# Crossings between the stages of a five-layer network: a weight split on GpSimd, tiles taken bank by bank, and the normalization folded into the turn

## The chip, the cores and the metric

The kernel runs on one core of a Trainium2 chip. The metric is the device time of one execution, in microseconds, as the median of the runs.

## The reference

A sequence of 256 tokens of 1024 features goes through four layers and then a fifth of another kind, all in 32-bit floats. Each layer is

```
h = h + 0.5 * rmsnorm(ffn(rmsnorm(h, g0)), g1)
h = h + rmsnorm(mixer(rmsnorm(h, g2)), g3)
h = h + 0.5 * rmsnorm(ffn(rmsnorm(h, g4)), g5)
```

with `ffn(x) = (silu(x @ w_gate) * (x @ w_up)) @ w_down` of 2816 hidden features, `rmsnorm(x, g) = x * rsqrt(mean(x*x) + eps) * g`, and as mixers a windowed attention (layers 0 and 3), a gated linear attention (GLA, layer 1) and an RWKV-7 time mix (layer 2). The fifth layer has the same three parts without the norm behind each (`h = h + 0.5 * ffn(rmsnorm(h, g))`) and a hybrid of two attentions as mixer; a last rmsnorm follows.

## The kernel before

Tokens lie on the partitions as two tiles of 128 (NT = 2). The sum h and the scratch y are held in SBUF, [128, 2, 1024]. To keep the precision of 32 bits every weight and every activation is split into a high part, rounded to the matmul's faster 32-bit type, and a low part (the rest), and each product is three matmuls. Weights stream in units through four raw buffers: SP issues the loads (`load_unit`, L292), ACT makes the high part (`split_high`, L264, the instruction at L269), DVE the low part (`split_low`, L271, at L273); two buffers hold split units. A raw buffer is free once `weights_split` counts its unit, and SP waits for that in order.

The work is a list of stages: "ffn" (23 units; each unit PE's gate and up matmuls at L337 and L338 and the down matmuls of the unit before at L350 to L352, tile 0 before tile 1, into four banks of PSUM, `out_banks`), "proj" (a matrix product in chunks of 256 columns, L481, into `gate_bank` or, for a mixer's last product, `out_banks`), attention and mixer stages, and "cross". Behind each stage `barrier` (L227) lets PE, ACT and DVE wait for one another except where `passes` (L234) says otherwise.

A crossing takes the result of the last product in `out_banks` (two banks a tile) to the input of the next. There are 16. 14 are turned, that is they end in a transpose: the first, which has no result to add; five behind a mixer's product; eight behind an ffn. The other two are the one into the RWKV mixer and the last. In a turned crossing with a gain:

- ACT squares tile 0 of the result and sums it (`root_of`, L549, square at L551, root at L552), then tile 1. DVE multiplies tile 1 by the gain (L610), then, once ACT has the root of tile 0, tile 0, so that the two are never at one bank. With a bias (behind attention) DVE adds it first (L601), ACT squares that sum in y, and DVE waits for ACT's drain before the gain product (L606).
- DVE: reciprocal and residual addition `h += y * rstd` (`residual`, L615, at L622) for tile 0, then tile 1. Without a norm the addition takes the result straight from PSUM (L624).
- ACT squares h for the next norm; DVE writes y = h * rstd (`normed`, L632, at L637).
- PE transposes each block of 128 columns of y with the identity (`cross_pe`, L676, at L681) into `out_banks`, eight for tile 0, then eight for tile 1.
- ACT writes the high part of x, scaled by the next gain, for each of eight blocks (L581); DVE the low part (L648). PE's next stage starts on block 0 when its low part is there.

At an ffn's end PE signals `branch_tile_ready` after the last matmul of tile 0 and `weights_used` after that of tile 1. ACT and DVE split the first unit of the next stage there (L383, L414), ahead of the crossing; where the crossing follows an ffn they have also split the first part of that stage's second unit (`split_early_high`, `split_early_low`). DVE starts such a crossing when all of the ffn's matmuls are done (L596). Behind a projection the barrier stands ahead of the crossing.

## Time and profile before

| | us |
|---|---|
| median of 3 runs | 3422.99 (3420.08 to 3426.07) |
| the profiled execution | 3428.41 |
| its span, first to last instruction | 3426.6 |

```profile
PE 2971.8 (87%) x17510; PEld 2595.5 (76%) x17510; DVE 1982.3 (58%) x2349; ACT 1435.1 (42%) x1781; POOL 0.9 (0%) x9
```

This line of the page gives each engine's busy time and its share of the span. PE is the matrix engine, PEld its weight loads, DVE the vector engine, ACT the scalar engine, POOL GpSimd; SP issues the weight loads. L numbers are lines of the kernel. In timelines a row names start, duration, engine, line, operation, output<-inputs with their shapes, a count, and in brackets how long the engine had been idle before and who released it. The granted clock of TensorE in that execution was 0.919 of full speed on the mean.

### The profile page before, as it was taken

What the parts mean: (1) busy time and instruction counts of PE and PEld (TensorE: products, weight loads), DVE (VectorE), ACT (ScalarE), POOL (GpSimd) and SP (SyncE); (2) the same over time, 40 slices, a digit from 0 to 9 for tenths busy, and PEclk for the clock granted to TensorE, in tenths of its full rate; (3) what the DMA queues carried; (4) which work ended last, traced back from release to release, by engine and by line L of the source; (5) the groups of instructions that cost most, each with busy time, mean ns of one, the idle gap of its engine ahead of it and who ended that gap; (6) DMA issues with size and microseconds to landing.
All of it is one profiled execution on the core that took longest, in us unless ns stands there. A gap on an engine that the chain in (4) does not pass through costs nothing.

```text
span 3426.6 us, 43921 instructions
## 1 busy us (share of the span) xinstructions
PE 2971.8 (87%) x17510; PEld 2595.5 (76%) x17510; DVE 1982.3 (58%) x2349; ACT 1435.1 (42%) x1781; POOL 0.9 (0%) x9
## 2 busy tenths in 40 slices
PE   6987898988589799666887898997799997978898
PEld 5876787878478688655885787886687886977887
DVE  4665666663756566655555566666566663645565
ACT  4444445443344444442221444445444443434443
POOL 0000000000000000000000000000000000000000
PEclk9997899998699999887997899999799998989999
DMA  7643565644056565320000565653365555642562
GB/s 224 184 129 99 159 189 175 184 129 148 1 172 190 145 201 166 110 86 1 1 1 20 154 184 162 202 164 106 117 184 177 177 166 138 180 132 83 176 192 92
DMA packets 639646, 471.49 MB, mean 138 GB/s; under 512 B 56002, under 2 KB 607298, under 8 KB 639509
## 3 DMA queue, kind: packets, MB, share of 16 engines
q1 hardware_dynamic: 609456, 451.00, 43.7%
q10 hardware_dynamic: 30052, 18.57, 2.2%
q8 instruction: 97, 1.59, 0.2%
q14 instruction: 41, 0.33, 0.0%
HBM read 466.63 MB, written 1.84 MB: 137 GB/s over the span
## 4 chain that ended last, share of the span: by engine, by line
PE 70%; DVE 14%; ACT 6%; PEld 4%; ACTq 3%; issue 2%; PEldq 1%; DVEq 1%; DMA 0%; SPq 0%
PE pair_bank L337 22%; PE pair_bank L338 11%; PE pair_bank L481 11%; PE out_banks L350 5%; PE out_banks L352 5%; PE out_banks L351 5%; PEld out_banks L481 3%; DVE low L273 2%; ACT high L269 2%; PEldq L229 1%; DVE mix L1896 1%; PE pair_bank L1737 1%; DVEq L229 1%; PE out_banks L681 1%; PE pair_bank L1750 1%
## 5 line engine op out<-in xcount | busy, mean ns | idle before, releaser
L273 DVE TENSOR_TENSOR low<-raw,high 128x3072 fp32r<-128x3072 f32 (+3 forms) x328 | 948.0, 2890 | 889.9 <-ACT high L269 889.9
L337 PE MATMUL pair_bank<-x_parts,high 128*128 128x512 f32 x3520 | 1247.9, 396 | 34.8 <-DVE low L273 29.6
L338 PE MATMUL pair_bank<-x_parts,low 128*128 128x256 f32 x3520 | 988.1, 281 | 0.0
L269 ACT ACTIVATE high<-raw 128x3072 fp32r<-128x3072 f32 (+3 forms) x328 | 784.9, 2393 | 402.3 <-PE out_banks L352 199.8
L337 PEld LDWEIGHTS pair_bank<-x_parts,high 128*128 128x128 f32 x3520 | 665.5, 189 | 194.8 <-DVE low L273 28.6
L338 PEld LDWEIGHTS pair_bank<-x_parts,low 128*128 128x128 f32 x3520 | 670.3, 190 | 9.3
L377 ACT ACTIVATE sq_scratch<-pair_bank 128x512 f32<-128x512 f32 x220 | 131.6, 598 | 580.4 <-PE pair_bank L338 580.4
L350 PE MATMUL out_banks<-high,hid_h 128*128 128x512 f32 x880 | 349.0, 397 | 13.0 <-DVE hid_l L411 13.0
L352 PE MATMUL out_banks<-high,hid_l 128*128 128x512 f32 x880 | 348.4, 396 | 0.0
L351 PE MATMUL out_banks<-low,hid_h 128*128 128x512 f32 x880 | 348.3, 396 | 0.0
L481 PE MATMUL pair_bank<-high,x_parts 128*128 128x256 f32 (+1 forms) x1248 | 245.7, 295 | 30.9 <-DVE low L273 17.0
L481 PE MATMUL pair_bank<-x_parts,high 128*128 128x256 f32 x1216 | 236.0, 296 | 40.2 <-DVEq L229 31.1
L481 PEld LDWEIGHTS pair_bank<-high,x_parts 128*128 128x128 f32 x1248 | 208.5, 203 | 34.4 <-DVE low L273 17.4
L481 PEld LDWEIGHTS pair_bank<-x_parts,high 128*128 128x128 f32 x1216 | 200.7, 203 | 44.6 <-issue 42.1
L350 PEld LDWEIGHTS out_banks<-high,hid_h 128*128 128x128 f32 x880 | 165.6, 188 | 56.7 <-DVE hid_l L411 9.3
L352 PEld LDWEIGHTS out_banks<-high,hid_l 128*128 128x128 f32 x880 | 165.7, 188 | 39.8
L351 PEld LDWEIGHTS out_banks<-low,hid_h 128*128 128x128 f32 x880 | 165.7, 188 | 29.9
L481 PE MATMUL pair_bank<-low,x_parts 128*128 128x256 f32 (+1 forms) x624 | 182.2, 292 | 0.0
L481 PE MATMUL pair_bank<-x_parts,low 128*128 128x256 f32 x608 | 177.8, 292 | 0.0
L379 ACT ACTIVATE silu<-sq_scratch 128x256 f32<-128x256 f32 x220 | 91.9, 418 | 183.9 <-DVE sq_scratch L402 183.9
L402 DVE TENSOR_TENSOR sq_scratch<-sq_scratch,pair_bank 128x512 f32<-128x512 f32 x220 | 151.2, 687 | 27.1 <-ACT sq_scratch L377 21.3
L405 DVE TENSOR_TENSOR hidden<-silu,sq_scratch 128x256 f32<-128x256 f32 x220 | 93.5, 425 | 106.5 <-ACT silu L379 106.5
(348 smaller groups left out, 3108.1 us busy)
## 6 DMA issues: line engine op xcount, KB each, us to landing
raw<-in_ffn_w_in_dram SPq DMA_DIRECT2D x352, 512.0 KB
raw<-in_ffn_w_out_dram SPq DMA_DIRECT2D x176, 512.0 KB
raw<-in_ffn_w_dram SPq DMA_DIRECT2D x132, 512.0 KB
raw<-in_w_in_dram SPq DMA_DIRECT2D x32, 1024.0 KB
raw<-in_gla_w_in_dram SPq DMA_DIRECT2D x12, 1024.0 KB
raw<-in_rwkv_w_rkv_dram SPq DMA_DIRECT2D x12, 1024.0 KB
raw<-in_swa_w_qkv_dram SPq DMA_DIRECT2D x10, 1024.0 KB
raw<-in_swa_w_o_dram SPq DMA_DIRECT2D x8, 1024.0 KB
```

The source lines that it names most:

```text
L269: nc.scalar.activation(high[u % SPLIT][:, lo:w], raw[u % RAW][:, lo:w], ACT.Copy).then_inc(high_ready, count)
L273: nc.vector.tensor_tensor(low[u % SPLIT][:, lo:w], raw[u % RAW][:, lo:w], high[u % SPLIT][:, lo:w].bitcast(F32), ALU.subtract).then_inc(we ...
L337: nc.tensor.matmul(o, H[:, w], x_parts[:, k, :], start=(k == 0), stop=False)
L338: last = nc.tensor.matmul(o[:, 0:SEQ], L[:, w], xh[:, k, :], start=False, stop=(k == KB - 1))
L350: nc.tensor.matmul(o, hid_h[b][:, tok], H[:, w], start=(q == 1), stop=False)
L351: nc.tensor.matmul(o, hid_h[b][:, tok], L[:, w], start=False, stop=False)
L352: last = nc.tensor.matmul(o, hid_l[b][:, tok], H[:, w], start=False, stop=(q == FB))
L377: nc.scalar.activation(lows[:, :, :], halves[:, :, SEQ:2 * SEQ], ACT.Copy).then_inc(lows_copied, 1)
L379: nc.scalar.activation(silu[:, :], sums[:, 0, :], ACT.Silu).then_inc(silu_ready, 1)
L402: nc.vector.tensor_tensor(sums[:, :, :], lows[:, :, :], halves[:, :, 0:SEQ], ALU.add).then_inc(sums_ready, 1)
L405: nc.vector.tensor_tensor(hidden[:, :], silu[:, :], sums[:, 1, :], ALU.mult).then_inc(hidden_made, 1)
L481: last = nc.tensor.matmul(o, a, b, start=(j == 0), stop=(j == len(terms) - 1))
```

## The change

- **Split on GpSimd.** In the eight turned crossings behind an ffn, DVE no longer makes the low part of the next stage's first unit; GpSimd does, as soon as ACT has the high part. DVE waits for it after its second `normed`, then drains and counts `weights_split`.
- **Tiles as they end.** All 13 turned crossings behind a product begin on tile 0 when PE has done it (`tile_wait`), without the barrier; the last chunk of a projection signals it too. Tile 1 follows with `weights_used`.
- **Bank by bank.** With a gain and no bias, DVE multiplies bank 0 of a tile while ACT squares bank 1, then they change over. DVE turns the sum of the one half into `half_mean`, and ACT's root takes this as its bias beside the sum of the other. The residual addition of tile 0 stands ahead of the second half of tile 1. This order also holds in the crossing into the RWKV mixer. With a bias, the drain is gone: DVE waits for the root instead.
- **The turn.** `normed` writes a diagonal matrix, identity times rstd, of 128 columns, and PE multiplies the blocks of h by it instead of transposing y.

The diff, cut to its core:

```diff
+        half_squares, half_mean = silu[:, 0:NT], hidden[:, 0:NT]
...
-            if st.kind == "ffn":
-                return then.kind == "cross" and then.turn
+            if tile_early(then):
+                return True
             if me == "pe" and then.kind == "proj" and then.x_wait is not None:
                 return True
             return me == "pe" and st.kind == "cross" and st.turn and then.kind in ("ffn", "proj")
+
+        def ends_in_tiles(st):
+            return st.kind == "ffn" or st.kind == "proj" and st.dest == "out"
+
+        def tile_early(st):
+            return st.kind == "cross" and st.turn and st.at > 0 and ends_in_tiles(stages[st.at - 1])
+
+        def tile_wait(eng, st, t):
+
+            if not tile_early(st):
+                return
+            last = stages[st.at - 1]
+            if t == 0:
+                eng.wait_ge(branch_tile_ready, len([x for x in stages[:st.at - 1] if ends_in_tiles(x)]) + 1)
+            else:
+                eng.wait_ge(weights_used, last.u0 + last.units)
+
+        def splits_first(st):
+            return after_ffn(st) and next_unit(st.at - 1) is not None
+
+        def firsts_before(st):
+            return len([x for x in crossings if x.at < st.at and splits_first(x)])
...
-                elif next_unit(st.at) is not None:
+                elif next_unit(st.at) is not None and not splits_first(stages[st.at + 1]):
                     split_low(dve, next_unit(st.at), words(next_unit(st.at)))
...
+                    elif st.dest == "out" and c == len(st.chunks) - 1 and x == 0:
+                        last.then_inc(branch_tile_ready, 1)
...
-        def root_of(act, src, slot, scale):
-
-            link_act(act, nc.scalar.activation(sq_scratch[:, :], src, ACT.Square, accum_out=squares[:, slot:slot + 1]))
+        def squares_of(act, src, total, at=0):
+
+            return nc.scalar.activation(sq_scratch[:, at:at + src.shape[-1]], src, ACT.Square, accum_out=total)
+
+        def root_of(act, slot, scale, offset):
             nc.scalar.activation(root[:, slot:slot + 1], squares[:, slot:slot + 1], ACT.Sqrt, scale=scale * scale / D,
-                                 bias=ln_eps[:, int(scale) - 1:int(scale)]).then_inc(root_ready, 1)
+                                 bias=offset).then_inc(root_ready, 1)
 
         def cross_act(act, st):
             post, pre = st.post, st.pre
             if st.post_gained:
-                if after_ffn(st):
-                    act.wait_ge(branch_tile_ready, stages[st.at - 1].nth + 1)
                 for t in range(NT):
                     if post.bias is not None:
                         biases[0] += 1
                         act.wait_ge(biased, biases[0])
-                    elif t == 1:
-                        free_turns[0] += 1
-                        act.wait_ge(tile_free, free_turns[0])
-                        if after_ffn(st):
-                            act.wait_ge(weights_used, stages[st.at - 1].u0 + FB + 1)
-                    root_of(act, y[:, t, :] if post.bias is not None else out_banks[:, t * D:(t + 1) * D], t, 1 / post.scale)
-                    if post.bias is not None:
-                        act.drain().then_inc(branch_read, 1)
+                        link_act(act, squares_of(act, y[:, t, :], squares[:, t:t + 1]))
+                        root_of(act, t, 1 / post.scale, ln_eps[:, int(1 / post.scale) - 1:int(1 / post.scale)])
+                    else:
+                        tile_wait(act, st, t)
+                        squares_of(act, out_bank[2 * t + 1][:, :], half_squares[:, t:t + 1], 512).then_inc(half_squared, 1)
+                        halves[0] += 1
+                        act.wait_ge(half_gained, halves[0])
+                        link_act(act, squares_of(act, out_bank[2 * t][:, :], squares[:, t:t + 1]))
+                        act.wait_ge(half_known, halves[0])
+                        root_of(act, t, 1 / post.scale, half_mean[:, t:t + 1])
+            if halves[0] > 0:
+                act.wait_ge(half_squared, halves[0])
             if pre is not None:
                 for t in range(NT):
                     if post is not None:
                         act.wait_ge(h_ready, posts_before(st) + t + 1)
-                    root_of(act, h[:, t, :], NT + t, 1)
+                    link_act(act, squares_of(act, h[:, t, :], squares[:, NT + t:NT + t + 1]))
+                    root_of(act, NT + t, 1, ln_eps[:, 0:1])
...
-            if after_ffn(st):
-                dve.wait_ge(weights_used, stages[st.at - 1].u0 + FB + 1)
-            if st.post_gained:
-                dve.wait_ge(gain_loaded[0], 16 * st.gains[0])
-                for t in range(NT):
-                    if post.bias is not None:
-                        v_.tensor_tensor(y[:, t, :], out_banks[:, t * D:(t + 1) * D], post.bias, ALU.add).then_inc(biased, 1)
-                for t in (range(NT) if post.bias is not None else (1, 0)):
-                    if post.bias is not None:
-                        bias_read[0] += 1
-                        dve.wait_ge(branch_read, bias_read[0])
-                        last = v_.tensor_tensor(y[:, t, :], y[:, t, :], gain[0][:, :], ALU.mult)
-                    else:
-                        if t == 0:
-                            dve.wait_ge(root_ready, roots + 1)
-                        last = v_.tensor_tensor(y[:, t, :], out_banks[:, t * D:(t + 1) * D], gain[0][:, :], ALU.mult)
-                        if t == 1:
-                            last.then_inc(tile_free, 1)
-                link(dve, last)
+
+            def gained_half(t, n):
+
+                cols = slice(512 * n, 512 * n + 512)
+                return v_.tensor_tensor(y[:, t, cols], out_bank[2 * t + n][:, :], gain[0][:, cols], ALU.mult)
+
+            def gained_first(t):
+                tile_wait(dve, st, t)
+                gained_half(t, 0).then_inc(half_gained, 1)
+
+            def gained_second(t):
+                halves_read[0] += 1
+                dve.wait_ge(half_squared, halves_read[0])
+                v_.tensor_scalar(half_mean[:, t:t + 1], half_squares[:, t:t + 1], 1 / post.scale / post.scale / D,
+                                 EPS / post.scale / post.scale, ALU.mult, ALU.add).then_inc(half_known, 1)
+                link(dve, gained_half(t, 1))
 
             def residual(t):
 
                 if post is None:
                     return
+                r = rstd[:, t:t + 1]
                 if st.post_gained:
                     dve.wait_ge(root_ready, roots + t + 1)
-                    link(dve, v_.reciprocal(rstd[:, t:t + 1], root[:, t:t + 1]))
-                    ins = v_.scalar_tensor_tensor(h[:, t, :], y[:, t, :], rstd[:, t:t + 1], h[:, t, :], ALU.mult, ALU.add)
+                    link(dve, v_.reciprocal(r, root[:, t:t + 1]))
+                    ins = v_.scalar_tensor_tensor(h[:, t, :], y[:, t, :], r, h[:, t, :], ALU.mult, ALU.add)
                 else:
+                    tile_wait(dve, st, t)
                     ins = v_.scalar_tensor_tensor(h[:, t, :], out_banks[:, t * D:(t + 1) * D], post.scale, h[:, t, :], ALU.mult, ALU.add)
                 ins.then_inc(h_ready, 1)
...
             def normed(t):
 
                 s = NT + t
+                r = rstd[:, s:s + 1]
                 dve.wait_ge(root_ready, roots + NT * st.post_gained + t + 1)
-                link(dve, v_.reciprocal(rstd[:, s:s + 1], root[:, s:s + 1]))
-                v_.tensor_scalar(y[:, t, :], (h if st.turn else y)[:, t, :], rstd[:, s:s + 1], None, ALU.mult).then_inc(y_ready, 1)
-
+                link(dve, v_.reciprocal(r, root[:, s:s + 1]))
+                if st.turn:
+                    v_.tensor_scalar(y[:, t, 0:P], ident[:, :], r, None, ALU.mult).then_inc(y_ready, 1)
+                else:
+                    v_.tensor_scalar(y[:, t, :], y[:, t, :], r, None, ALU.mult).then_inc(y_ready, 1)
+
+            if st.post_gained:
+                dve.wait_ge(gain_loaded[0], 16 * st.gains[0])
+                if post.bias is not None:
+                    for t in range(NT):
+                        tile_wait(dve, st, t)
+                        v_.tensor_tensor(y[:, t, :], out_banks[:, t * D:(t + 1) * D], post.bias, ALU.add).then_inc(biased, 1)
+                    for t in range(NT):
+                        dve.wait_ge(root_ready, roots + t + 1)
+                        link(dve, v_.tensor_tensor(y[:, t, :], y[:, t, :], gain[0][:, :], ALU.mult))
+                else:
+                    gained_first(0)
+                    gained_second(0)
+                    gained_first(1)
             residual(0)
+            if st.post_gained and post.bias is None:
+                gained_second(1)
             if pre is None or st.turn:
                 residual(1)
                 if st.turn:
                     normed(0)
                     normed(1)
+                    if splits_first(st):
+                        dve.wait_ge(first_low, firsts_before(st) + 1)
+                        dve.drain().then_inc(weights_split, 1)
                     dve.wait_ge(columns_loaded[st.turned0 % 2], 16 * (st.turned0 // 2 + 1))
...
-                    ins = nc.tensor.transpose(out_bank[k // 2][:, at:at + P], y[:, t, k * P:(k + 1) * P], ident[:, :])
+                    ins = nc.tensor.matmul(out_bank[k // 2][:, at:at + P], h[:, t, k * P:(k + 1) * P], y[:, t, 0:P],
+                                           start=True, stop=True)
...
+            for st in crossings:
+                if splits_first(st):
+                    u, w = next_unit(st.at - 1), words(next_unit(st.at - 1))
+                    pool.wait_ge(high_ready, u + 1)
+                    nc.gpsimd.tensor_tensor(low[u % SPLIT][:, 0:w], raw[u % RAW][:, 0:w],
+                                            high[u % SPLIT][:, 0:w].bitcast(F32), ALU.subtract).then_inc(first_low, 1)
 
```

## Rows read from the trace of the kernel before

**Rows 1.** The page's chain that ended last, shares of the span by engine.

```profile
PE 70%; DVE 14%; ACT 6%; PEld 4%; ACTq 3%; issue 2%; PEldq 1%; DVEq 1%; DMA 0%; SPq 0%
```

**Rows 2.** Timeline of DVE, 549 to 559: start us, us, instruction, idle before.

```profile
549.42 2.29 DVE L273 TENSOR_TENSOR low<-raw,high 128x2048 fp32r<-128x2048 f32 x1 [2.11 <-ACT high L269]
551.92 2.36 DVE L610 TENSOR_TENSOR y<-out_banks,gain 128x1024 f32<-128x1024 f32 x2 [0.21 <-issue]
...
556.03 1.29 DVE L622 SCALAR_TENSOR_TENSOR h<-y,rstd,h 128x1024 f32<-128x1024 f32 x1
...
557.61 0.75 DVE L637 TENSOR_SCALAR y<-h,rstd 128x1024 f32<-128x1024 f32 x1
```

**Rows 3.** Timeline of ACT in the same crossing.

```profile
549.51 1.03 ACT L551 ACTIVATE sq_scratch<-out_banks 128x1024 f32<-128x1024 f32 x1
550.43 0.19 ACT L551 ACTIVATION_READ_ACCUMULATOR sq_scratch<-out_banks 128x1 f32 x1
550.65 0.29 ACT L552 ACTIVATE root<-squares,ln_eps 128x1 f32<-128x1 f32 x1
```

**Rows 4.** Timeline of PE in the same crossing.

```profile
548.70 0.40 PE L352 MATMUL out_banks<-high,hid_l 128*128 128x512 f32 x1
...
550.10 0.40 PE L352 MATMUL out_banks<-high,hid_l 128*128 128x512 f32 x1
558.42 3.67 PE L681 MATMUL out_banks<-ident,y 128*128 128x128 f32 x16 [7.92 <-DVE y L637]
```

**Rows 5.** Groups by line: out<-in, count, busy us, mean ns, idle before.

```profile
L681 PE MATMUL out_banks<-ident,y 128*128 128x128 f32 x224 | 51.1, 422 | 115.2 <-DVE y L637 115.2
```

**Rows 6.** Chain in order of time (start us, us, what), behind one crossing.

```profile
362.57 2.78 ACT high L269
365.47 3.37 DVE low L273
```

**Rows 7.** Groups by line, shapes apart: count, busy us, mean ns, idle before.

```profile
L402 DVE TENSOR_TENSOR sq_scratch<-sq_scratch,pair_bank 128x512 f32<-128x512 f32 x220 | 151.2, 687 | 27.1 <-ACT sq_scratch L377 21.3
...
L1160 DVE TENSOR_SCALAR mix<-mix 128x128 f32<-128x128 f32 x32 | 7.0, 283 | 0.3
...
L377 ACT ACTIVATE sq_scratch<-pair_bank 128x512 f32<-128x512 f32 x220 | 131.6, 598 | 580.4 <-PE pair_bank L338 580.4
```

**Rows 8.** Windows: busy of PE, PEld, DVE, ACT, POOL, granted clock, DMA.

```profile
347.00:348.00 1.00, 0.00 (x0) 0.00 (x0) 0.47 (x2) 0.85 (x4) 0.00 (x0) 0.62 1.18 310
...
555.00:556.00 1.00, 0.00 (x0) 0.00 (x0) 0.96 (x2) 0.17 (x1) 0.00 (x0) 0.72 1.15 301
...
867.00:868.00 1.00, 0.87 (x4) 0.90 (x5) 0.98 (x1) 0.00 (x0) 0.00 (x0) 0.50 0.00 0
```

**Rows 9.** Timeline of PE in the GLA mixer, plain matmuls.

```profile
867.13 2.05 PE L1318 MATMUL out_banks<-y,mix 128*128 128x128 f32 x8 [18.95 <-DVE mix L1342]
```

**Rows 10.** Timeline of DVE and PE at four other crossings.

```profile
341.16 2.29 DVE L273 TENSOR_TENSOR low<-raw,high 128x2048 fp32r<-128x2048 f32 x1 [3.47 <-ACT high L269]
...
354.88 3.65 PE L681 MATMUL out_banks<-ident,y 128*128 128x128 f32 x16 [10.01 <-DVE y L637]
...
960.67 2.29 DVE L273 TENSOR_TENSOR low<-raw,high 128x2048 fp32r<-128x2048 f32 x1 [3.47 <-ACT high L269]
964.46 1.22 DVE L610 TENSOR_TENSOR y<-out_banks,gain 128x1024 f32<-128x1024 f32 x1 [1.50 <-PEq L229]
...
2850.01 2.48 DVE L624 SCALAR_TENSOR_TENSOR h<-out_banks,h 128x1024 f32<-128x1024 f32 x2
...
3218.48 2.48 DVE L624 SCALAR_TENSOR_TENSOR h<-out_banks,h 128x1024 f32<-128x1024 f32 x2 [1.50 <-PEq L229]
```

**Rows 11.** Timeline of POOL, its last instructions of the run.

```profile
0.92 0.10 POOL L846 MEMSET ln_eps<- 128x1 f32 x1
0.95 0.20 POOL L847 MEMSET ident<- 128x128 f32 x1
1.39 0.29 POOL L849 TENSOR_SCALAR_AFFINE_SELECT ident<-ident 128x128 f32<-128x128 f32 x1 [0.23 <-POOL ident L847]
```

More of the change, by code:

```diff
@@ L195, in build @@
         biased = sem("biased")
-        tile_free = sem("tile_free")
-        branch_read = sem("branch_read")
+        half_gained = sem("half_gained")
+        half_known = sem("half_known")
+        half_squared = sem("half_squared")
+        first_low = sem("first_low")
         root_ready = sem("root_ready")
@@ L587, in build @@
         biases = [0]
-        free_turns = [0]
-        bias_read = [0]
+        halves = [0]
+        halves_read = [0]
         def cross_dve(dve, st):
```

## The prediction

> **What bounds the kernel now.** I read the page's chain of waits first [rows 1]. It is 70% PE, yet 14% of it lies on DVE and 6% on ACT. The reader is to see that the matmuls set the pace only inside a stage; between stages something else does. So the next view is the timeline of one crossing, engine by engine, here from the second matrix of a feed-forward stage to the next feed-forward stage [rows 2 to 4]. PE's last matmul starts at 550.10 and lasts 0.40, so PE stops at 550.5. It works again at 558.42, when the 16 transposes start, after 7.92 us without work [rows 4]. All of that gap is a single thread on DVE and ACT. DVE is bound up with the low half of the next weights until 551.71 (549.42 + 2.29) although tile 1 was done at 550.5; then 2.36 us of gain products, two residual additions of 1.29, and a normalized copy of 0.75 [rows 2]. ACT's squares hang in between [rows 3]. There are 14 such crossings, 224 transposes at 16 each [rows 5].
>
> Does time won in a crossing reach the end? Behind a crossing ACT and DVE split the next unit only when the crossing's last DVE work is done: in the one that starts a feed-forward stage after attention ACT's split starts at 362.57 and DVE's at 365.47, which ends at 368.8, and PE waits for it [rows 6]. Those pieces shift with the crossing's end, so I count a saving in a crossing in full.
>
> **The change, part by part.** Prices: a product of a PSUM half (512 columns) takes DVE 0.69, ACT reads one in 0.60, and a 128x128 scaling takes DVE 0.28 where the 128x1024 one took 0.75 [rows 2, 7]. Reading ACT's accumulator lands about 0.1 us beyond the square and the root takes 0.29 [rows 3]; a one-column instruction on DVE takes 0.16, with some 0.04 us between linked ones.
>
> (a) *Diagonal matrix instead of the normalized copy*: 0.75 becomes 0.28 on the thread, 0.47 us in each turned crossing. In exchange PE runs a plain 32-bit matmul of 128 columns instead of a transpose. With the clock at 0.50 [rows 8] eight plain ones took 2.05 us [rows 9], and sixteen transposes 3.67 [rows 4]. Less one duration of 0.42 [rows 5] that is 0.23 and 0.22 from start to start, so I take this at nothing. Were each 0.1 us dearer, eight in a row would cost 0.8 us a crossing, 11 us in 14; that is the other end.
>
> (b) *Feed-forward to a turned crossing with gain* (7 of them). I rerun the thread with DVE free. Tile 0 is done six matmuls before PE's stop, at 549.1. DVE: first half 549.15 to 549.84, one-column mean after ACT's first square (ACT is free when DVE's split could start, 549.4; square 549.51 to 550.1, sum at 550.2) 550.3 to 550.46, second half to 551.19, first half of tile 1 (ready 550.5) 551.23 to 551.92, reciprocal, residual 0 from 552.16 to 553.45, then mean and second half of tile 1 to 554.35, residual 1 to 555.85, reciprocal and diagonal matrix to 556.38. PE starts at 556.43 instead of 558.42: 1.99 us. Its eight products of tile 0 last until 558.3, and the second diagonal matrix is there at 557.9 (squares of h 555.9 to 557.0, root 557.35), so nothing new is late. 7 x 1.99 = 13.9.
>
> (c) *Feed-forward into the hybrid mixer* (no gain): DVE did both residuals from 2850.01 [rows 10], behind the same split. Now it starts at 2847.3, when tile 0 is ready: 2.7 + 0.47 = 3.2.
>
> (d) *Projection to crossing*. The barrier goes and tile 0, ready about 2.9 us (24 matmuls) earlier, is used while PE does tile 1. DVE still has its own split to do first. After attention (2 crossings with a bias) that ends at 343.45 [rows 10]; the bias sums then run 343.5 to 344.7 and 344.9 to 346.15, the root of tile 0 is there at 346.25, the gain products end at 347.5 and 349.0, the residuals at 350.5 and 352.0, the diagonal matrix at 352.5. PE starts at 352.6 instead of 354.88 [rows 10]: 2.3 each, 4.6. After the two mixers without bias DVE is free at 962.96 and its first product waited until 964.46 [rows 10]; the same working as in (b) from 963.0 gives PE's start at 969.9 instead of 971.4: 1.5 each, 2.9 for both. Out of the hybrid mixer the residuals waited 1.50 behind the split [rows 10] and now start 1.46 earlier: 1.9 with (a).
>
> (e) *First crossing*: (a) alone, 0.5. *Feed-forward to the crossing that isn't turned*: it keeps its barrier but gets the halves, which cost extra fixed parts: 0.7 us lost. The last crossing is as before.
>
> (f) *The split on POOL* (8 crossings). What waits: DVE, just ahead of the low parts of x, for POOL; and SP, queued behind the count that DVE now gives after the second diagonal matrix. SP's next weights are issued at about 558 rather than 551.7; but the unit they bring is the fifth of the stage, and those of the four ahead of it lie in their buffers. I cost that at nothing; without that cover it would be up to 6 us a crossing. POOL begins at 549.45. No row shows POOL with such a subtraction. From its rows: memory fills take 0.10 for one column and 0.20 for 128, which scaled gives 1.7 us for 2048 columns; the select of 128x128 takes 0.29, sixteen of them 4.6 [rows 11]; and as a subtraction reads two operands, twice that, 9.2, is the far end. I take 4.6, the row that reads, computes and writes. POOL is then done at 554.05, well ahead of DVE's need at about 559.
>
> The sum: 0.5 + 13.9 + 3.2 + 4.6 + 2.9 + 1.9 - 0.7 = 26.3 us.
>
> (g) *What POOL does to DVE.* On this kernel POOL stands idle from 1.7 us on [rows 11], so no row has the two side by side. The residual addition 0 is DVE's first instruction in the crossing whose two tensors both lie in SBUF (y and h), as POOL's two do; the ones before it take one from PSUM. If it can't read beside POOL it starts at 554.05, not 552.16: 1.9 us late, and everything behind it is late by as much, since the thread has no slack (ACT's root for tile 1 hangs on DVE's mean, which is queued behind this addition). 7 x 1.9 = 13.3. Into the hybrid mixer the additions read PSUM; there the diagonal matrix, wanted at 2850.35, waits until 2852.2: 1.8. Together 15.1, which leaves 26.3 - 15.1 = 11.2. I take this as the likeliest: two engines with two operand streams each must both be fed out of the same memory for whole instructions, and nothing shown excludes it.
>
> The Trainium skill (SBUF — State Buffer, section "Who interferes with whom") says that a DVE instruction with two SBUF inputs contends with a GpSimd instruction that reads SBUF, and that the later one blocks fully; by that rule the forecast is the 11.2, and without it 26.3. No run here shows it yet. The Trainium skill (GPSIMD Engine Reference, section "Performance versus the Vector engine") gives 4497 ns for an fp32 tensor_tensor of 2048 columns; with that the wait would be 1.8 us and the sum 12.
>
> **Rivals.** *Forecast*: POOL takes about 4.6 and blocks the two-input instructions. Against the profiled execution (3428.4 with its 3426.6 span) 3417.2; that execution lies 5.4 above the median of the runs, so on the median 3422.99 - 11.2 = 3411.8. For d between 4.0 and 5.2 it moves by 8 x 0.6 = 5 us either way.
> *POOL and DVE don't meet*, or POOL takes under 2.7 us: the whole 26.3, 3396.7. For: nothing in the trace speaks against; against: both read the same memory.
> *POOL blocks every DVE instruction*: the mean at 550.3 waits until 554.05 (3.75 each), in the hybrid's crossing the second residual from 2848.7 to 2852.2 (3.5): 26.3 - 26.3 - 3.5 = -3.5, 3426.5.
> *Slower: POOL takes longer and holds the additions*. With 9.2 us, two operands each at the select's rate, the additions wait 6.5 us in 7 crossings and the matrix 6.4 in one: 51.9, which is 25.6 slower, 3448.6. It decides from d = 2.7 + 26.3 / 8 = 6.0 us on.
> *The crossings shorten and it doesn't show*: PE's clock fell to 0.50 within about 3 us of a stop in one place and 5 in another [rows 4, 8, 10] and is low again behind the stalls after a crossing; with other phases 14 crossings could lose what they win, or plain matmuls could be dearer as in (a). About 3421.
>
> **Chances.** Forecast 0.50, no meeting 0.27, all of DVE blocked 0.08, doesn't show 0.08, slower 0.07. A difference under 0.2% (6.8 us) can't be told from none. Faster: the first two but for the forecast's upper edge, 0.75; same 0.17; slower 0.08. The range reaches from 4 us under the no-meeting case, 3392, to 3424, which leaves out the two cases above; the phases of the clock are worth some 4 us, inside it. The likeliest one's own range is 3405 to 3418.
>
> **What would show it.** POOL with 8 subtractions starting when ACT's split ends: their length is d. DVE idle ahead of residual 0 in the 7 crossings shows (g); gap or none tells forecast from rival, and idle ahead of the mean instead shows the third. PE's gap in (b) should be 5.9 us without waiting and 7.8 with, in the hybrid's crossing 2.0 or 3.8 instead of 5.2, after attention 7.7 instead of 10. The diagonal products should take as long as the transposes. Wrong it would be with d far from 4.6, with DVE waiting for POOL ahead of the low parts of x, or with PE waiting for weights at the fifth unit of a stage.

## The result, and the profile after

The changed kernel takes 3445.82 us (median of 4 runs, 3440.49 to 3449.56) where the kernel before, measured beside it, takes 3422.3 (4 runs, 3420.08 to 3426.07): the ratio is 1.0066, 95% interval 1.0049 to 1.0084. It is some 23 us slower. The prediction said 3411.8, faster, with 3424 as its upper edge, so it was wrong in sign and range. The profiled execution took 3445.29 with a span of 3443.2, 16.6 us more than the span of before.

The page's chain of the kernel after, by engine, answers to [rows 1]:

```profile
PE 73%; DVE 14%; ACT 6%; ACTq 3%; issue 2%; DVEq 1%; PEldq 1%; PEld 0%; DMA 0%; SPq 0%
```

DVE's share is what it was, although its thread was to become shorter; PE has more. Now the same crossing as in [rows 2 to 4]. First DVE:

```profile
554.10 0.15 DVE L651 RECIPROCAL rstd<-root 128x1 f32<-128x1 f32 x1
554.29 3.27 DVE L652 SCALAR_TENSOR_TENSOR h<-y,rstd,h 128x1024 f32<-128x1024 f32 x1
...
558.58 1.28 DVE L652 SCALAR_TENSOR_TENSOR h<-y,rstd,h 128x1024 f32<-128x1024 f32 x1
...
560.10 0.29 DVE L670 TENSOR_SCALAR y<-ident,rstd 128x128 f32<-128x128 f32 x1
```

POOL's subtraction of this crossing:

```profile
551.94 4.53 POOL L909 TENSOR_TENSOR low<-raw,high 128x2048 fp32r<-128x2048 f32 x1 [329.87 <-ACT high L294]
```

And PE and ACT at the turn:

```profile
552.57 0.39 PE L377 MATMUL out_banks<-high,hid_l 128*128 128x512 f32 x1
560.44 5.93 PE L734 MATMUL out_banks<-y,h 128*128 128x128 f32 x32 [7.48 <-DVE y L670]
```

```profile
565.13 3.04 ACT L613 ACTIVATE x_parts<-out_banks,gain_columns 128x256 fp32r<-128x256 f32 x8 [3.76 <-PE out_banks L734]
```

The reader is to see two things. Residual 0 (L652, the addition h<-y,rstd,h of tile 0) takes 3.27 us beside POOL, residual 1 takes 1.28 behind it: the hold that step (g) forecast. And the turn is a row of x32 and 5.93 us, where [rows 4] has x16 and 3.67. There are 16 products in it, 8 for each tile, so each leaves two records. ACT's first block comes 565.13 - 560.44 = 4.69 us behind the turn's start; before it came at 560.91, 2.49 behind 558.42. The page's group of that line counts 448 records over the run (it answers to [rows 5]), for 224 products:

```profile
L734 PE MATMUL out_banks<-y,h 128*128 128x128 f32 x448 | 88.6, 388 | 100.9 <-DVE y L670 100.9
```

Adding up all 14 turned crossings from PE's last product ahead of each to the last low part of x behind it, before has 208.3 us and after 224.2: 15.9 of the 16.6 us lie in the crossings. The stages between them sum to 3218.3 and 3219.0. From the turn's start to the last low part before takes 6.6 to 6.7 us in every crossing, and after 8.8 to 8.9 in 13 of the 14 (7.86 in the last).

### The profile page after: what moved, and what is told of

Read it like the earlier page. It is cut to its first block, busy times and chain, and to the rows that moved or that the text cites. A ratio compares the mean times of both kernels' runs of the same rounds, so it can differ in the third digit from the quotient of the medians.

```text
span 3443.2 us, 44483 instructions
## 1 busy us (share of the span) xinstructions
PE 3003.1 (87%) x17734; PEld 2631.1 (76%) x17734; DVE 1970.6 (57%) x2381; ACT 1438.5 (42%) x1821; POOL 37.2 (1%) x17
## 4 chain that ended last, share of the span: by engine, by line
PE 73%; DVE 14%; ACT 6%; ACTq 3%; issue 2%; DVEq 1%; PEldq 1%; PEld 0%; DMA 0%; SPq 0%
PE pair_bank L362 22%; PE pair_bank L363 11%; PE pair_bank L506 11%; PE out_banks L375 5%; PE out_banks L377 5%; PE out_banks L376 5%; PE out_banks L506 3%; ACT high L294 3%; DVE low L298 2%; PE out_banks L734 2%; DVE mix L1956 1%; DVE h L652 1%; PE pair_bank L1797 1%; PEldq L232 1%; DVEq L232 1%
## 5 line engine op out<-in xcount | busy, mean ns | idle before, releaser
L298 DVE TENSOR_TENSOR low<-raw,high 128x3072 fp32r<-128x3072 f32 (+2 forms) x320 | 929.7, 2906 | 875.0 <-ACT high L294 875.0
L734 PE MATMUL out_banks<-y,h 128*128 128x128 f32 x448 | 88.6, 388 | 100.9 <-DVE y L670 100.9
```

Of the source, the lines that this page charges most:

```text
L298: nc.vector.tensor_tensor(low[u % SPLIT][:, lo:w], raw[u % RAW][:, lo:w], high[u % SPLIT][:, lo:w].bitcast(F32), ALU.subtract).then_inc(we ...
L734: ins = nc.tensor.matmul(out_bank[k // 2][:, at:at + P], h[:, t, k * P:(k + 1) * P], y[:, t, 0:P], start=True, stop=True)
```

## Experiments

The theory at this point: the plain product is what costs, about 2.2 us a crossing on the way to ACT's first block, and everything else of the change brings close to nothing because POOL takes back what the earlier tiles give. The rival: the new order of tiles, or POOL, does the harm. I tell the crossings by the one shown above. "Gap" is PE's time without work ahead of the turn (behind the idle matmuls, where a kernel has them), "to ACT" the time from the turn's start to ACT's first block:

| kernel | gap | to ACT | median us | ratio to before [95%] |
|---|---|---|---|---|
| before | 7.92 | 2.49 | 3422.3 | 1 |
| after | 7.48 | 4.69 | 3445.82 | 1.0066 [1.0049, 1.0084] |
| turned_back | 7.92 | 2.49 | 3421.72 | 0.9987 [0.9978, 0.9996] |
| diagonal_alone | 7.45 | 4.55 | 3450.61 | 1.0073 [1.0059, 1.0086] |
| tiles_alone | 8.24 | 2.49 | 3419.43 | 0.9987 [0.9977, 0.9996] |
| split_in_gap | 5.94 | 2.49 | 3414.19 | 0.9965 [0.9951, 0.9979] |
| pool_fill | 5.95 | 2.49 | 3410.56 | one run |
| pool_copy | 5.95 | 2.49 | 3406.89 | one run |
| pool_fill_thrice | 5.95 | 2.49 | 3411.63 | one run |
| pool_copy_thrice | 7.82 | 2.49 | 3424.06 | one run |
| filled | 1.00 | 2.04 | 3410.45 | 0.9952 [0.9938, 0.9965] |
| diagonal_filled | 0.56 | 2.60 | 3405.50 | 0.9938 [0.9924, 0.9952] |
| after_filled | 2.62 | 4.22 | 3430.46 | 1.0013 [1.0004, 1.0022] |
| before_filled | 3.00 | 2.49 | 3430.28 | 1.0008 [0.9999, 1.0017] |

The kernel before read 3426.02 beside the first four experiments, 3427.84 beside the next four and 3427.49 beside the last four; times of different groups are best compared by their ratios.

**The diagonal matrix, undone and alone.** turned_back is the kernel after with

```diff
-v_.tensor_scalar(y[:, t, 0:P], ident[:, :], r, None, ALU.mult).then_inc(y_ready, 1)
+v_.tensor_scalar(y[:, t, :], h[:, t, :], r, None, ALU.mult).then_inc(y_ready, 1)
...
-ins = nc.tensor.matmul(out_bank[k // 2][:, at:at + P], h[:, t, k * P:(k + 1) * P], y[:, t, 0:P],
-                       start=True, stop=True)
+ins = nc.tensor.transpose(out_bank[k // 2][:, at:at + P], y[:, t, k * P:(k + 1) * P], ident[:, :])
```

> The changed kernel with the turn as before: the normalized copy of 1024 columns and PE's transposes instead of the diagonal matrix and plain products; POOL's split and the early tiles stay. Theory A (each plain 32-bit product runs as two passes, so 16 of them are 32 records and the first pair of blocks reaches ACT 2.2 us later): from the start of the turn to ACT's first block 2.5 us again, PE's gap 7.9 us behind a feed-forward stage, and the time some 24 us under the changed kernel, about 3415 to 3422. Theory B (POOL's subtraction, with what waits for it, is the loss; plain products cost what transposes cost): within 7 us of the changed kernel, about 3445.

diagonal_alone is the kernel before with the opposite edit.

> The kernel before with the diagonal matrix and the plain products alone. Theory A: 14 crossings at 2.2 - 0.47 = 1.75 us each slower, 24 us, about 3446. Theory B: 14 x 0.47 = 6.6 us faster, about 3416.

Both come out by Theory A. Undone, the whole loss is gone: 0.9987 instead of 1.0066. Alone, it costs 1.0073, about 25 us, as much as the whole change loses. PE's turn of diagonal_alone, and the same stretch by windows (columns: busy time of PE, PEld, DVE, ACT and POOL with their instructions, granted clock, DMA share, GB/s):

```profile
559.92 5.80 PE L684 MATMUL out_banks<-y,h 128*128 128x128 f32 x32 [7.45 <-DVE y L638]
```

```profile
560.00:562.00 2.00, 2.00 (x10) 2.00 (x10) 0.45 (x2) 0.76 (x3) 0.00 (x0) 0.50 0.02 6
562.00:564.00 2.00, 2.00 (x11) 2.00 (x11) 0.00 (x0) 0.00 (x0) 0.00 (x0) 0.50 0.00 0
564.00:565.80 1.80, 1.72 (x15) 1.52 (x14) 0.39 (x1) 1.33 (x4) 0.00 (x0) 0.98 0.00 0
```

The turn starts 0.47 us earlier behind PE's last product (7.45 against 7.92), as predicted, and its first 4 us run at a granted clock of 0.50 (1.2 GHz) and hold some 20 of the 32 records. The records cost about what a transpose costs; there are twice as many. The Trainium skill (FP8 and Floating Point Precision, section "TensorE Precision Notes") has true FP32 go through the array in 4 passes. The trace shows two records for each product, as long from start to start as a transpose's one (0.23 and 0.22 us, [rows 9, 4]); how many passes stand behind a record it doesn't show.

**The tiles without POOL.** tiles_alone is turned_back with POOL's block taken out and the split put back on DVE at the old place.

```diff
-elif next_unit(st.at) is not None and not splits_first(stages[st.at + 1]):
+elif next_unit(st.at) is not None:
...
-if splits_first(st):
-    dve.wait_ge(first_low, firsts_before(st) + 1)
-    dve.drain().then_inc(weights_split, 1)
```

> The changed kernel with the turn as before and without POOL's split: DVE makes the first low part at its old place. Early tiles and the order bank by bank alone. Theory A: behind a projection 1.4 us earlier each (5 of them), behind a feed-forward stage with gain about 0.5 us later each (7, the halves cost fixed parts and DVE starts as late as before), about 3419. Theory B: the early tiles win what was forecast of them, and POOL took it away: about 3410.

split_in_gap, too, is turned_back without POOL's block, but DVE makes the split behind its second normalized copy, where turned_back waited for POOL.

```diff
-    dve.wait_ge(first_low, firsts_before(st) + 1)
-    dve.drain().then_inc(weights_split, 1)
+    split_low(dve, next_unit(st.at - 1), words(next_unit(st.at - 1)))
```

> As tiles_alone, but DVE makes the first low part behind its second normalized copy, where the changed kernel has it wait for POOL, in the 2 us in which it waits for the turn. Theory A: PE's gap behind a feed-forward stage about 6.4 us, no addition longer than 1.3 us, some 0.4 us given back where the low parts of x start; crossings with gain 1.1 us shorter than before, about 3406. Theory B with POOL gone: the same gap, so this run does not tell A from B; it tells whether the early tiles win anything once nothing stands in front of them (if not, about 3422).

tiles_alone gains as little as turned_back. Its gap in this crossing is even 0.3 us longer than before, since DVE's split still comes first and the halves add fixed parts. split_in_gap gets 0.9965: its 14 crossings sum to 185.4 us, 22.9 less than before. Yet its span, 3410.6, is only 16.0 less. The other 6.9 are in the stages between (3225.2 against 3218.3). I had expected a gap of about 6.4 us and 3406; the gap is shorter, 5.94, and the time longer, 3414.19. PE's first product of the next stage, in the kernel before and in split_in_gap:

```profile
562.49 0.47 PE L337 MATMUL pair_bank<-x_parts,high 128*128 128x512 f32 x1 [0.39 <-DVE x_parts L648]
```

```profile
555.43 0.77 PE L362 MATMUL pair_bank<-x_parts,high 128*128 128x512 f32 x1 [0.52 <-DVE x_parts L700]
```

and the windows over the same place, of before, of split_in_gap and of pool_fill (told below; its gap is as short, 5.95):

```profile
562.60:566.00 3.40, 3.40 (x19) 2.72 (x20) 2.48 (x7) 1.34 (x4) 0.00 (x0) 1.00 0.00 0
```

```profile
555.00:560.00 5.00, 4.57 (x14) 3.92 (x15) 3.03 (x8) 1.76 (x5) 0.00 (x0) 0.50 0.84 224
```

```profile
554.30:559.30 5.00, 4.99 (x25) 4.37 (x26) 2.61 (x7) 1.47 (x5) 0.00 (x0) 0.90 0.94 296
```

Before, PE's clock was back at 1.00 when the stage began; in split_in_gap its first 5 us still run at 0.50. It is so behind all seven feed-forward stages with gain: the first 5 us of the next stage have a mean clock of 0.50 to 0.58 in split_in_gap and of 0.80 to 1.00 before. Over the 14 crossings the first 31 products behind the turn take 78.4 us before and 88.1 in split_in_gap, enough for the 6.9. That is the part of the fifth rival ("doesn't show") that is real. The shorter stop alone doesn't do it, though: pool_fill stops as briefly, yet its mean clocks there are 0.81 to 1.00 and its first 31 products sum to 78.7 us. Its stage starts 0.39 us behind the turn's end and split_in_gap's 0.52, with DVE's split ahead of the low parts; whether that decides it, no run shows.

**What of POOL holds DVE?** Four kernels on turned_back with POOL's subtraction replaced: by a fill (below), by a copy (tensor_copy of the same raw tensor into low), and by three of each, with a drain behind each one. The low half of those weights is then not computed.

```diff
-nc.gpsimd.tensor_tensor(low[u % SPLIT][:, 0:w], raw[u % RAW][:, 0:w],
-                        high[u % SPLIT][:, 0:w].bitcast(F32), ALU.subtract).then_inc(first_low, 1)
+nc.gpsimd.memset(low[u % SPLIT][:, 0:w].bitcast(F32), 0.0).then_inc(first_low, 1)
```

> turned_back with POOL's subtraction replaced by a memory fill of the same 2048 columns, which reads nothing (the low part of eight units of weights is left out, zero in its place). If the wait of DVE's addition comes of two engines reading SBUF, residual 0 takes 1.3 us again and PE's gap behind a feed-forward stage is 6.4 us or less, though POOL runs at the same place. If it comes of POOL running at all, or of its writes, the addition stays at 3.3 us where the fill is as long as the subtraction (4.5 us); the fill's length itself is open, 1.7 us by the scaling of the small fills.

> turned_back with POOL's subtraction replaced by a copy of the raw weights, one SBUF input (the low part of eight units is wrong by the high part, left in). If any read of POOL holds DVE's two-input addition, the addition ends with the copy, whatever its length, and one that would start behind the copy's end takes 1.3 us. If only POOL's second input does it, 1.3 us in each crossing.

Single fills (1.81 us) and copies (1.90 us) end before residual 0 begins. Both gave a gap of 5.95 here and could not tell reading from writing; they only showed that a short POOL instruction is hidden. So three in a row:

> The same with three fills of 1.8 us each: GpSimd only writes, and the low half of these weights is zero. If reading is what holds DVE's addition, it keeps its 1.29 us and the fills their 1.8, with a total near pool_fill's 3410.6 or below. If any access of GpSimd does it, this looks like pool_copy_thrice: additions or fills that take about 1 us longer in 7 crossings.

> The kernel turned_back with GpSimd's subtraction replaced by three copies of the same tensor, one after the other, some 1.9 us each and 5.7 together, so that GpSimd is still at work when DVE adds residual 0, but reads one tensor, not two. The low half of these weights is then left uncomputed. If any GpSimd instruction that reads SBUF holds DVE's two-input addition, the addition (1.29 alone) takes longer by what is left of the copy beside which it starts, or GpSimd's next copy is held in its turn and takes over 2.5. If only two read streams collide with two, both keep their lengths, and the total is near pool_copy's 3406.9.

Residuals 0 and 1 on DVE, and POOL beside them, of pool_fill_thrice:

```profile
545.69 1.28 DVE L652 SCALAR_TENSOR_TENSOR h<-y,rstd,h 128x1024 f32<-128x1024 f32 x1
...
547.99 1.28 DVE L652 SCALAR_TENSOR_TENSOR h<-y,rstd,h 128x1024 f32<-128x1024 f32 x1
```

```profile
543.32 5.65 POOL L909 MEMSET low<- 128x2048 f32 x3 [321.28 <-ACT high L294]
```

and of pool_copy_thrice:

```profile
547.93 2.64 DVE L652 SCALAR_TENSOR_TENSOR h<-y,rstd,h 128x1024 f32<-128x1024 f32 x1
...
551.59 1.80 DVE L652 SCALAR_TENSOR_TENSOR h<-y,rstd,h 128x1024 f32<-128x1024 f32 x1
```

```profile
545.57 6.75 POOL L909 CAST low<-raw 128x2048 fp32r<-128x2048 f32 x3 [323.03 <-ACT high L294]
```

Beside fills both additions keep their 1.28 us; beside copies they take 2.64 and 1.80, and of the three copies the first two take 1.90 and 1.89 us and the third, which starts while residual 0 is under way, 2.70. It is the same in all seven such crossings (each kernel ran once). So POOL's reading of SBUF holds DVE's two-input addition, one read stream is enough, its writing alone doesn't hold it, and the hold works both ways. The gap is 7.82 against 5.95: 7 x 1.87 = 13 us, and the spans differ by 3421.9 - 3409.2 = 12.7. By the Trainium skill (SBUF — State Buffer, section "Who interferes with whom") a DVE instruction with two SBUF inputs contends with a GpSimd instruction that reads SBUF and not with one that only writes it; these two runs agree with both halves of that.

DVE's other instruction of a crossing, the normalized copy with its one SBUF input, behaves otherwise. It meets POOL only in the crossing into the hybrid mixer, here in pool_fill_thrice:

```profile
2829.60 1.50 DVE L670 TENSOR_SCALAR y<-h,rstd 128x1024 f32<-128x1024 f32 x1
...
2831.20 2.19 DVE L670 TENSOR_SCALAR y<-h,rstd 128x1024 f32<-128x1024 f32 x1
```

```profile
2826.82 6.02 POOL L909 MEMSET low<- 128x2048 f32 x3 [191.09 <-ACT high L294]
```

Alone it takes 0.75. Beside POOL's fills, which only write, the two copies take 1.50 and 2.19 us, and the third fill 2.17 instead of 1.81. So it isn't true of every DVE instruction that POOL's writing leaves it alone; this one crossing, in one execution, is all that shows it.

**Is the product dear at any clock?** filled is split_in_gap with idle matmuls on PE ahead of the turn, their results unread, so that PE doesn't stand still in the crossing:

```diff
 def cross_pe(pe, st):
+    if st.post is not None:
+        for _ in range(8 if not st.post_gained else 20 if st.post.bias is None else 32):
+            nc.tensor.matmul(pair_bank[0][:, 0:512], x_parts[:, 0, 0:P], x_parts[:, 0, :], start=True, stop=True)
```

> split_in_gap with 20 idle matmuls of 512 columns on PE behind each product stage (32 with the bias, 8 without gain), into a bank that nobody reads, so that PE's gap is short and its clock stays at the upper level. If what split_in_gap gives back (crossings 22.9 us shorter, time 12 shorter) is the clock at the head of the next stage, the turn reaches ACT after about 1.4 us instead of 2.5, the next stage's first unit runs at full clock, the stages are 7 us and more shorter in sum, and the time is 3385 to 3400. If it is the later weight loads or something on ACT and DVE, the stages stay as long and only the turn gains: 13 x 1.1, about 3400 to 3405. If PE's fill gets in the way of the turn, slower.

diagonal_filled adds the diagonal matrix and the plain products to it.

> filled with the diagonal matrix and the plain products. Theory A: two passes per product, now at full clock: from the start of the turn to ACT 2.4 us where the transposes take 1.4, against 0.47 us won on DVE: 13 crossings at about 0.5 us slower, 7 us behind filled. If the price of the plain products at low clock was something else than passes (starting cost, the first product), the two differ by less than 2 us or the diagonal one is ahead.

PE of filled and of diagonal_filled at the turn:

```profile
551.08 1.09 PE L736 MATMUL out_banks<-ident,y 128*128 128x128 f32 x8 [1.00 <-DVE y L670]
552.58 1.09 PE L736 MATMUL out_banks<-ident,y 128*128 128x128 f32 x8 [0.41 <-DVE y L670]
```

```profile
545.51 4.82 PE L731 MATMUL pair_bank<-x_parts 128*128 128x512 f32 x20
550.88 3.84 PE L736 MATMUL out_banks<-y,h 128*128 128x128 f32 x32 [0.56 <-DVE y L670]
```

and the windows of diagonal_filled, with the clock at 1.00 throughout:

```profile
545.30:550.80 5.50, 4.92 (x21) 3.67 (x20) 5.26 (x10) 4.03 (x12) 0.00 (x0) 1.00 0.01 3
550.80:555.00 4.20, 3.84 (x32) 3.65 (x32) 3.14 (x6) 2.50 (x8) 0.00 (x0) 1.00 0.00 0
```

filled misses its own expectation (3385 to 3400): it takes 3410.45. Its stages sum to 3219.7 us in the profiled execution, 5.5 less than split_in_gap's, so most of the 6.9 is the clock at their heads; but its crossings sum to 183.4, only 2 less. Behind the seven feed-forward stages with gain the last low part comes 6.79 us behind the turn's start in filled as in split_in_gap, at either clock, because DVE's split stands ahead of the low parts.

With PE at full clock the 32 records reach ACT in 2.60 us instead of 4.69, only 0.56 more than transposes (2.04), which the earlier diagonal matrix (0.45) nearly pays for: both kernels' crossings sum to the same within 1 us (119.3 and 118.4, counted from the end of the idle matmuls). In part the split hides the products here, since diagonal_filled has those 6.79 us too. Behind attention, where no split stands there, the last low part comes 6.09 us behind the turn's start with transposes and 6.77 with products: 0.68 dearer at full clock, against 2.2 at the low one. I had expected diagonal_filled behind filled; it is not: 3405.50 (3404.70 to 3406.46) against 3410.45 (3405.13 to 3412.96), with overlapping intervals of the ratios. What I had overlooked is that at full clock the transposes' turn waits for the second normalized copy (the 0.41 above), not for PE. diagonal_filled beats the kernel before by 0.6% and is the best version I ran, though its lead over filled isn't sure.

**The idle matmuls on the two kernels themselves.**

> The changed kernel, whole, with one addition: 32 (with a bias 20, without gain 8) matmuls of 512 columns whose results nobody reads, on PE behind the last product of the stage ahead of each crossing, so that PE's clock is still up when the turn's 32 records come. If the plain products are dear only because the clock has fallen when they run, turn to ACT's first block goes from 4.7 us to about 2.6 as in diagonal_filled, 13 times 2.1 = 27 us less than the changed kernel, of which the earlier split of diagonal_filled is no part: near 3405.5 + 7.5 (turned_back less split_in_gap, what GpSimd costs against DVE in the gap) = 3413. If the products are dear at any clock (two passes that the crossing feels), it stays above 3430. The addition of DVE beside GpSimd stays at about 3.3 us in both cases.

> The kernel before with the same idle matmuls ahead of its crossings, nothing else changed: what the clock alone is worth to it. The gap is 7.9 us there and the idle matmuls fill some 7 of it. If the clock is what they buy, 16 transposes and their way to ACT take 2.0 us rather than 2.5 and the head of the next stage runs at full clock: near 3418 (3422.3 less the 3.7 that filled won on split_in_gap) or somewhat lower, down to 3413. If what diagonal_filled won over before came mostly from the gap's own edits, this stays within 5 us of before.

Both expectations missed: 3430.46 instead of 3413, and 3430.28, no faster than before, instead of 3413 to 3418. Still, after_filled is some 18 us faster than after (1.0013 against 1.0066), and its crossings are 18.0 us shorter in sum (206.2 against 224.2): with the clock up in part of the crossings most of the change's loss is gone. In after_filled POOL's hold (residual 0 takes 3.35 us) leaves a gap of 2.62 us behind the idle matmuls, in before_filled the old thread leaves 3.00. Two crossings of after_filled with the same gap, turn by windows:

```profile
557.60:562.00 4.40, 4.40 (x25) 4.40 (x26) 0.45 (x2) 1.08 (x4) 0.00 (x0) 0.61 0.37 107
```

```profile
757.00:760.50 3.50, 3.50 (x31) 3.50 (x32) 0.45 (x2) 1.80 (x6) 0.00 (x0) 1.00 0.18 32
```

After the same stop of 2.62 us the clock fell in one, 0.4 us behind the start of the turn, and not in the other. One turn reached ACT in 4.22 us, the other in 2.59: in one kernel, with the same instructions, the granted clock alone makes 1.6 us. It was low in 5 of the 7 crossings with this stop and in none of the other 6, whose stops are 1.48 us and less. In before_filled, with stops of 1.67 to 3.00 us, the clock was 1.00 from the turn's start to ACT's first block in 3 of 13 crossings. Its crossings are 2.8 us shorter than before's (205.5) and its stages 7.0 longer, 5.8 of them in the one stage behind the crossing into the hybrid mixer; what lengthened that one I didn't trace. I had taken the clock to survive gaps of 3 us; it did so after every stop up to 1.48 us and not reliably after 2.62, and in before_filled it was low behind one of 1.86.

## Why the prediction was wrong, step by step

**(a), the failed step.** "Less one duration ... that is 0.23 and 0.22 from start to start, so I take this at nothing." The division was right and its unit wrong: the x8 of [rows 9] are eight records, not eight products. The code of that line issues four there (four heads, one tile at level 0), which with the count would have shown two records for each (the line leaves 136 records in the run for the 68 products it issues). So a product takes 0.46 us at that clock, twice a transpose, and both ends of my bound were too low: even the dear end, 0.1 us each, was under half of it. Measured: +2.2 us on the way to ACT in a crossing at low clock (4.69 against 2.49), less the 0.47 gained on DVE, is +1.7, by 14 some 24 us; diagonal_alone shows about 25. I had -6.6 (14 x 0.47). That difference of some 31 us is nearly the whole error: 3411.8 + 31 = 3443. The rival that named dearer products had 0.08 and 3421, because I priced it by a guess and not by a row that shows a lone product. The sign that I had named for it, "The diagonal products should take as long as the transposes", is the one that failed: 5.93 us against 3.67.

**(b) to (e), the earlier tiles, right.** Where POOL doesn't hold DVE (split_in_gap) the gap in (b) is 5.94 with copies; I had 5.9 with the diagonal matrix, so the thread is some 0.4 us better than my rerun. With POOL I had 7.8 and after shows 7.45 to 7.52. The gaps of the others:

| crossing | before | forecast | after |
|---|---|---|---|
| into the hybrid mixer | 5.21 | 3.8 | 3.65 |
| out of it | 4.10 | 2.2 | 2.16 |
| attention (two) | 10.01 | 7.7 | 7.95, 8.31 |
| mixers without bias | 7.01 | 5.5 | 5.13 |

The crossing of (e) that isn't turned loses 0.17 us (PE's gap 11.82 instead of 11.65), not the 0.7 of the sum.

**(f) and (g), POOL, right.** The subtraction takes 4.53 us in all 8 crossings (I took 4.6 from the select of [rows 11]). Residual 0 is held for 3.27 - 1.28 = 1.99 us, forecast 1.9, and neither DVE nor PE is seen waiting for POOL ahead of x's low parts. That the later weight loads of (f) cost nothing agrees with the stages' sums, 3218.3 and 3219.0. In the crossing into the hybrid mixer POOL works until 2862.92, and DVE shows:

```profile
2858.05 1.23 DVE L655 SCALAR_TENSOR_TENSOR h<-out_banks,h 128x1024 f32<-128x1024 f32 x1 [1.82 <-PE out_banks L377]
2859.53 1.23 DVE L655 SCALAR_TENSOR_TENSOR h<-out_banks,h 128x1024 f32<-128x1024 f32 x1 [0.25 <-PE out_banks L377]
...
2861.15 1.86 DVE L670 TENSOR_SCALAR y<-ident,rstd 128x128 f32<-128x128 f32 x1
...
2863.12 0.29 DVE L670 TENSOR_SCALAR y<-ident,rstd 128x128 f32<-128x128 f32 x1
```

The additions that read PSUM are free beside POOL, as assumed; the diagonal matrix is held until POOL's end, as assumed. The rival of the whole of DVE blocked falls with the one-column instructions, which keep their 0.15 us, and the one of POOL at 9.2 us with the 4.53.

**The sum, mended.** Without (a)'s 6.6 my 11.2 is 4.6, and turned_back, which is the change without (a), is 0.13% faster, 4.5 us (interval 1 to 8). So the terms beside (a) held in sum. That the two meet so closely is in part luck: turned_back's turned crossings are 8.1 us shorter than before's (200.2 against 208.3), where my terms for them, without (a), give 5.3; the thread is better than my rerun, and not all that it wins reaches the end. Of the 26.3 - 6.6 = 19.7 us that I gave the rival without a meeting, split_in_gap shows 12 (0.35%, interval 7 to 17), because of the second step that was off: "I count a saving in a crossing in full". There the low clock at the head of the next stage took 6.9 of 22.9 us back. The single runs of pool_fill and pool_copy, whose heads weren't so slow, lie 17 and 21 us below the kernel before.

## What to carry to other kernels

Before a row of one profile prices an instruction, divide its count by what the code issues at that place: a plain 32-bit matmul leaves two records here and costs two, a transpose leaves one. Work moved to another engine isn't free if both read SBUF; splitting the same weights on DVE behind the second normalized copy, where DVE had time, beat GpSimd by about 0.2% (0.9965 against 0.9987). PE's clock can stay low into the stage behind a crossing (split_in_gap) though an equal stop in another kernel doesn't leave it so (pool_fill), so count the windows' clock on both sides of a stop, not the stop alone.

## What the runs showed of the hardware that I had not expected

A plain 128x128 product of 32-bit tensors costs two records of about 0.23 us each at a granted clock of 0.50. DVE's scaling of one SBUF tensor is also held by POOL: 1.86 us instead of 0.29 beside its subtraction, 1.50 and 2.19 instead of 0.75 beside its fills. A copy on POOL is itself lengthened by DVE's addition, from 1.90 to 2.70 us. Idle matmuls that end up to 1.5 us ahead of the turn kept the clock at 1.00 through it in every such crossing of filled, diagonal_filled and after_filled; those that end 2.6 us ahead did so in 2 of 7. And behind plain products the next stage starts at a clock of 1.00 in all 14 crossings of after, where before has a mean of 0.80 to 0.85 over the first 5 us in 8 of them: the first 31 products take 71.3 us in sum instead of 78.4. That doesn't show in the time, since the stages sum to 3219.0 and 3218.3. Whether diagonal_filled would win more with ACT's loads of gains and constants issued later, I didn't try: in filled PE then waits 1.49 us at 571.71 for DVE's split, which stands behind them.
